# Low halves of the second feed-forward's down weights: from GpSimd subtractions to negated copies on ScalarE and accumulating DMAs

## What is computed

```
x = x + (1.0 + g1[:, None, :]) * rms_norm(y, post_norm_mix[l])
h = modulate(rms_norm(x, pre_norm_mlp[l]), sh2, sc2)
y = jnp.square(jax.nn.relu(h @ w_ff1[l])) @ w_ff2[l]      # w_ff1 1024 x 4096, w_ff2 4096 x 1024
x = x + (1.0 + g2[:, None, :]) * rms_norm(y, post_norm_mlp[l])
```

## Time and profile before

| what | us |
|---|---|
| three runs: median (lowest to highest) | 1814.74 (1811.52 to 1820.94) |
| the profiled execution | 1814.2 |
| its span, first to last instruction | 1812.5 |
| PE busy in the span | 1765.2 (97%) |
| POOL busy | 1037.3 (57%) |
| ACT busy | 780.8 (43%) |
| POOL's 1124 subtractions at L1003 | 911.6 |

### The profile page before, as it was taken

How to read it: one execution, slowest core, us unless ns; L and a number is a source line. 1 busy time by engine, 2 the same in 40 slices (tenths; PEclk the granted TensorE clock), 3 DMA queues, 4 the chain that set the end, 5 groups by cost and what they waited for, 6 DMA issues and landing times. The chain is left out here.

```text
span 1812.5 us, 26067 instructions
## 1 busy us (share of the span) xinstructions
PE 1765.2 (97%) x8977; PEld 1440.3 (79%) x8977; DVE 1122.1 (62%) x1826; ACT 780.8 (43%) x1270; POOL 1037.3 (57%) x1265
## 2 busy tenths in 40 slices
PE   8999999999999999999999999999999999999998
PEld 6876888888888886788888888877666778988886
DVE  4788656566656338766666655644476567655665
ACT  5434543333334335453333333466566663333332
POOL 6574445555465557364555554457311558888885
PEclk9999999999999999999999999999999999999999
DMA  7221224443423221133444332413201112233221
GB/s 253 94 102 50 82 82 151 150 151 115 150 93 117 93 98 54 48 105 112 144 162 148 130 115 82 140 49 118 92 1 48 47 47 94 94 117 114 96 93 47
DMA packets 103206, 184.70 MB, mean 102 GB/s; under 512 B 7322, under 2 KB 67404, under 8 KB 101068
## 3 DMA queue, kind: packets, MB, share of 16 engines
q1 hardware_dynamic: 102940, 183.44, 28.8%
q10 hardware_dynamic: 176, 0.07, 0.0%
HBM read 180.35 MB, written 2.10 MB: 101 GB/s over the span
## 5 line engine op out<-in xcount | busy, mean ns | idle before, releaser
L1003 POOL TENSOR_TENSOR w_lo<-raw,w_hi 128x256 fp32r<-128x256 f32 (+1 forms) x1124 | 911.6, 845 | 751.0 <-ACT w_hi L1089 747.5
L2499 PE MATMUL ps<-n_hi,w_hi 128*128 128x512 f32 (+1 forms) x1320 | 507.1, 384 | 3.9 <-ACT zc L1394 1.8
L2501 PE MATMUL ps<-n_hi,w_lo 128*128 128x512 f32 (+1 forms) x1320 | 501.1, 380 | 0.0
L2500 PE MATMUL ps<-n_lo,w_hi 128*128 128x512 f32 (+1 forms) x1320 | 500.7, 379 | 0.0
L1089 ACT ACTIVATE w_hi<-raw 128x1024 fp32r<-128x1024 f32 (+2 forms) x331 | 307.8, 937 | 359.6 <-PE ps L2501 240.8
L2499 PEld LDWEIGHTS ps<-n_hi,w_hi 128*128 128x128 f32 x1320 | 249.0, 189 | 53.1 <-issue 6.0
L2501 PEld LDWEIGHTS ps<-n_hi,w_lo 128*128 128x128 f32 x1320 | 249.0, 189 | 48.0
L2500 PEld LDWEIGHTS ps<-n_lo,w_hi 128*128 128x128 f32 x1320 | 249.3, 189 | 45.4 <-issue 0.2
L2043 DVE TENSOR_TENSOR ps<-ps,sq 128x512 f32<-128x512 f32 x88 | 61.3, 699 | 179.8 <-PE ps L2501 177.4
L2499 PE MATMUL ps<-x_hi,w_hi 128*128 128x512 f32 x416 | 167.0, 401 | 0.1
L2501 PE MATMUL ps<-x_hi,w_lo 128*128 128x512 f32 x416 | 162.6, 391 | 0.0
(11 more groups left out here) (359 smaller groups left out, 2668.5 us busy)
## 6 DMA issues: line engine op xcount, KB each, us to landing
raw<-in_w_up SPq DMA_DIRECT2D x44, 1024.0 KB, 6.9
raw<-in_w_ff SPq DMA_DIRECT2D x32, 1024.0 KB, 6.6
raw<-in_w_in SPq DMA_DIRECT2D x26, 1024.0 KB, 6.1
zb<-in_ada_w SPq DMA_DIRECT2D x16, 1536.0 KB, 8.3
raw<-in_w_down SPq DMA_DIRECT2D x44, 512.0 KB, 3.9
raw<-in_w_out SPq DMA_DIRECT2D x12, 1024.0 KB, 6.1
raw<-in_w_in SPq DMA_DIRECT2D x4, 512.0 KB, 8.2
za<-in_x SPq DMA_DIRECT2D x4, 512.0 KB, 6.1
```

Source lines behind the costliest of these rows:

```text
L1003: last = pool.tensor_tensor(part[0], part[1], part[2], ALU.subtract)
L2499: pe.matmul(out, l_hi, r_hi, start=start, stop=False)
L2500: pe.matmul(out, l_hi, r_lo, start=False, stop=False)
L2501: return pe.matmul(out, l_lo, r_hi, start=False, stop=stop)
```

## The change

For the 32 quarters of the eight ff2 stripes, POOL no longer subtracts. ACT, behind each high half, also writes the negated high half into `w_lo` (the same rounding copy with scale -1). POOL then issues a DMA inside SBUF that adds the raw weights to it (`accum_op=ALU.add`, 128 partitions x 2 rows of 512 float32, 512 KB), and waits for the DMA of the quarter before; a memset of one column of a new small tile `mark` then counts that quarter in `wlo_ready`. Two semaphores take turns for the DMAs. All other quarters are made as before.

```diff
--- before.py
+++ after.py
@@ -547,6 +547,7 @@
         t_const = sb("t_const", [P, 2 * S], F32R)
         sb("rest_of_const", [P, NCONST - P - 2 * S])
         swapped = sb("swapped", [P, 2, S])
+        mark = sb("mark", [P, 8])
         banks = ctx.enter_context(nc.psum_tensor("ps", [P, 8 * S], F32))
         ps = [banks[:, i * S:(i + 1) * S] for i in range(8)]
 
@@ -555,6 +556,7 @@
         free = [sem(f"free{i}") for i in range(8)]
         landed = [sem(f"landed{i}") for i in range(2)]
         whi_ready, wlo_ready = sem("whi_ready"), sem("wlo_ready")
+        wneg_ready, wadd_in = sem("wneg_ready"), [sem(f"wadd_in{i}") for i in range(2)]
         quarter_done = sem("quarter_done")
         ada_in, ada_used = sem("ada_in"), sem("ada_used")
         ident_in, consts_in, pos_in = sem("ident_in"), sem("consts_in"), sem("pos_in")
@@ -738,6 +740,9 @@
 
             return free[4 + i % 4], BK.ffn2[4 + i % 4] + 2 * (FG2 - 1) + i // 4 + 1
 
+        added_at = {g: n for n, g in enumerate(st.at[q] for st, q in by_quarter if st.kind == "H" and st.index >=
+                                               STR["ff2", 0].index)}
+
         def landed_value(st):
             return 32 * (st.index // 2 + 1)
 
@@ -978,12 +983,27 @@
             pool.memset(fgw[:, :, :], 1.0).then_inc(ones_set, 1)
             pool.memset(blkw[:, :, :, :], 0.0).then_inc(blk_zero, 1)
             pool.memset(swapped[:, :, :], 0.0).then_inc(swap_zero, 1)
+            def added(n):
+
+                pool.wait_ge(wadd_in[n % 2], 16 * (n // 2 + 1))
+                pool.memset(mark[:, n % 8:n % 8 + 1], 0.0).then_inc(wlo_ready, 1)
+
             def lo(g, value, used, pieces=range(LO_PARTS)):
 
                 st, q = by_quarter[g]
                 if st.kind == "S" and q == 6:
                     pool.wait_ge(last_lo, (st.index - STR["ff1", SEVEN_FROM].index) // 2 + 1)
                     pool.memset(small[:, 42:43], 0.0).then_inc(wlo_ready, 1)
+                    return
+                if g in added_at:
+                    n = added_at[g]
+                    pool.wait_ge(wneg_ready, n + 1)
+                    pool.dma_start(split_quarter(st.kind, w_lo.bitcast(F32), g % 4, q), source(st, q), accum_op=ALU.add)\
+                        .then_inc(wadd_in[n % 2], 16)
+                    if q:
+                        added(n - 1)
+                    if q == st.quarters - 1:
+                        added(n)
                     return
                 if pieces[0] == 0:
                     if used is not None:
@@ -1088,6 +1108,9 @@
                     act.wait_ge(quarter_done, used)
                 act.activation(split_quarter(st.kind, w_hi, g % 4, q), source(st, q),
                                ACT.Copy).then_inc(whi_ready, 1)
+                if g in added_at:
+                    act.activation(split_quarter(st.kind, w_lo, g % 4, q), source(st, q), ACT.Copy, scale=-1.0)\
+                        .then_inc(wneg_ready, 1)
 
             def ensure(upto):
                 for g in range(ahead[0], min(upto, len(by_quarter))):
```

## The result

The changed kernel took 1911.04 us (median of 4 runs, 1908.11 to 1918.02), the kernel before 1814.75 us (4 runs, 1811.52 to 1820.94): a ratio of 1.0532, 95% interval 1.0490 to 1.0574. The forecast was 1842.2 in a range of 1814 to 1862. The sign was right; the loss is 96 us where 28 were forecast. The profiled run was the longest of the four, 1918.0 us with a span of 1916.1, 103.6 more than the span before.

The account below looks back on a forecast made before the run. PE, busy for 1765.2 of the 1812.5 us span, was taken to bound the kernel. Losses of 6 x 4.4 + 1.6 = 28.0 us on the profiled 1814.2 gave 1842.2, 1.5% slower; range 1814 to 1862.

Parts of the forecast that it names:

- The step that failed: In an ff2 stripe, POOL issues quarter 0's DMA at 1712.8 and quarter 1's at 1714.4, once its negated copy is ready.
- when the data of an addition start: Beside SP's load, quarter 0's data start 1.36 us after issue, at 1714.1, and it is marked at about 1719.4.
- A load that goes first: Sign in the profile after: a gap above 3 us at PE's first matmul means this or a slow issue.
- rival B: Additions take 3.84 us of data each, or the load is served first: 7.0 us a period, 1860 us; chance 0.25.
- The data of an addition, 2.56 us: Each 512 KB accumulating DMA reads source and destination, so its data take 2.56 us where one pass takes 1.28.
- ACT costs nothing: The 32 negated copies on ACT, about 1.0 us each, fit into idle time of 1.75 us or more: cost 0.
- No gain in freed time of POOL: Removing 128 POOL subtractions, 12.98 us a period, frees nothing PE waits for; gain at most 2.5 us or 0.14%.
- 4.4 us for each of stripes 1 to 6: PE's loss in each such ff2 period: quarter 1 marked at 1724.5 against 1720.06, with 0.7 us late at quarter 0 included.
- The 0 for stripe 0: ff2 stripe 0 follows an ordinary ff1 stripe, so its negated copies are ready far earlier and it loses 0.
- Stripe 7: Last ff2 stripe, behind another ff2 stripe: quarter 3 lands at 1792.3 against 1790.75, 1.6 us late; quarters 0 and 1 have time.
- A, no change: The DMAs are as cheap as copies, 1.28 us of data each, so marks come in time: 1814.4 us; chance 0.19.
- C, the clock: Each 4.4 us stall brings PE 10 us at granted clock 0.83: 10 us on top, 1852 us; chance 0.06.

Follow-up runs that it names:

- long rows: Changed kernel with each addition taking 128 rows of 4 KB in place of 256 rows of 2 KB, the same 512 KB: 1865.8 us.
- the first experiment: Changed kernel with the addition left out, so the 32 DMAs of POOL are plain copies of the weights: 1848.4 us.
- the kernel with 14 additions and no stall: Changed kernel with additions only for quarters 2 and 3 of ff2 stripes 0 to 6, POOL subtracting the rest: 1815.35 us, ratio 0.9998.

## Why the prediction was wrong

**The step that failed** is "POOL issues the DMA of quarter 0 at 1712.8 ..., that of quarter 1 at 1714.4 (negated copy)". It let a second DMA out while the first was under way, with nothing but ACT's copy to wait for. The second was held until the first had landed, and the mark of quarter 0 behind it too. Of the 96 us, the hold is some 45: with it gone (long rows) the time is 1865.8 in place of 1911.0. These are single runs, and it depends on what is taken away first: with the load already moved the long rows give 48 (1877.3 against 1829.5), and by the losses against the kernel before on each chip it is 42 and 51. I had asked what the issue costs on POOL, between 0 and 3.25 us; it costs 1.21. I had not asked how many could be out at once.

**The second is when the data of an addition start** ("with equal shares and data from 1712.8 + 1.36 = 1714.1: quarter 0 has its 2.56 at 1719.2 and is marked at about 1719.4", 6.6 us after its issue). It was marked 11.9 us after. The DMA queues of the changed kernel from 1726 to 1730 us, and from 1730 to 1734 us (packets, MB, share of the 16 engines):

```profile
q1 hardware_dynamic: 516, 1.03, 92.0%
q0 software_dynamic: 1, 0.00, 0.3%
```

```profile
q0 software_dynamic: 240, 0.49, 65.7%
q1 hardware_dynamic: 301, 0.61, 43.9%
```

In the first four microseconds the load moved alone, at 259 GB/s where the kernel before moves 359 in the same four after its issue (1714.5 to 1718.5). The addition's packets come from about 1730 on, some 5.8 us after the issue and not 1.36. Once both ran, the share was even: 64 packets and 0.13 MB for each queue in every microsecond from 1731 to 1734. So of the 5.3 us by which the mark was later than forecast, 4.4 lie ahead of the first packets. "A load that goes first" stands in the prediction among what would show it wrong, but the prices put it under rival B. It isn't the adding and not the number of packets: the plain copy issued at 1586.30 beside the load has its first packets after 1591, the addition in long rows issued at 1592.44 after 1597. With no load beside it, the addition issued at 1599.34 is under way from 1601 on.

The Trainium skill, "DMA: Bandwidth & Descriptors", section "Queues, rings and completion order", says that each DMA engine takes turns between the queues that it has work for, packet by packet. The second stretch is in keeping with it (240 and 301 packets). The first (1 and 516) would speak against it only if the addition's packets were already waiting at the engines, which no run shows. Why a DMA of POOL starts so late beside a load wasn't tried and stays open.

The load beside the additions is worth some 36 us, 1865.8 against 1829.5 with it moved away (34 with the hold in place, 1911.0 against 1877.3; 39 and 30 by the losses on each chip).

**What was right.** *The data of an addition, 2.56 us.* Alone, an addition of 512 KB takes 3.66 us from the end of its issue to its mark (1.21 issue; 1747.63 to 1752.51 above). Alone, a plain copy takes 2.37, by its rows in the first experiment:

```profile
1509.10 0.73 POOL L1001 DMA_DIRECT2D w_lo<-raw  x1 [5.39 <-ACT w_lo L1112]
...
1512.20 0.10 POOL L989 MEMSET mark<- 128x1 f32 x1 [2.25 <-DMA w_lo<-raw]
```

The difference is 1.29 us, one more pass of 1.28; with the 1.36 fixed I had 3.92 where 3.66 was measured. By the rule of the two source reads, which the prediction cites from the Trainium skill, "Collectives: The Full Stack", section "The bandwidth ceiling: the fold count and why AG ≠ RS ≠ AR", an addition moves data half as fast as a copy, and the rows agree: 211 GB/s in a microsecond inside an addition alone (1738 to 1739 in the changed kernel), 418 inside this copy (1510.5 to 1511.5). *ACT costs nothing*, and the copies were ready when forecast: two activations of 1.06 and 1.04 us behind one another, with idle time left; the ratio of 1.0007 shows it. *The load starts in the same microsecond* (SP's issue at 1724.38, POOL's at 1724.25). *No gain in freed time of POOL*: the kernel with 14 additions and no stall has a ratio of 0.9998.

**The sum, term by term.** 4.4 us for each of stripes 1 to 6 was 8.7 to 10.1 us of wait, 54.7 together, and the slower clock behind it. Where the second DMA isn't held, PE's gaps are 4.12 and 0.36 us in one of the periods and some 4.9 on average (35.2 us in all, less 2.0 at stripe 0 and 3.8 at stripe 7, over six). That this is near 4.4 is luck: the forecast had 0.7 us in front of quarter 0 and 3.7 in front of quarter 1, it is the other way round, and the clock isn't in it. The 0 for stripe 0 was wrong: 5.7 us. Its copies were indeed ready early, but POOL issued the first DMA only at 1500.40, beside that stripe's load, and nothing in the prediction looked at when POOL gets there. Stripe 7 lost 6.0 us of wait, not 1.6, and 2.51 of them in front of quarter 1, which the forecast had at nothing:

```profile
1883.41 0.47 PE L2522 MATMUL ps<-w_hi,n_hi 128*128 128x512 f32 x1 [2.51 <-POOL mark L989]
```

The mark of quarter 1 stands behind the issue of quarter 2, which waited until 1881.94 for ACT's copy, and ACT for its slot. That is the order of the program and not the hold: with long rows, where nothing is held, the same wait is 2.11 us. The 1.43 us in front of quarter 2 are the hold: the issue of quarter 3, and the mark of quarter 2 behind it, waited for quarter 2 to land, and with long rows PE doesn't wait there. In front of quarter 3 it is 2.05 us, and 1.72 with long rows, where 1.6 was forecast: that term was right.

**The rivals.** A, no change, fell. B, three passes or a load served first, is partly what happened (its load, not its three passes), at 7.0 a period; its 1860 is close to the 1865.8 without the hold, but that run has the slower clock in it too, so the nearness proves nothing. C, the clock, was given 0.06 and came true in every period: PE stood still for 6 us and the granted clock went to 0.50, not to the mean of 0.83 of the earlier trace rows. Its price of 10 us on top is within the 8 to 14 that keeping the clock up gave back, by luck: the clock was lower than it assumed, and part of the slow matmuls cost nothing. The error there was the chance, since the forecast's own gap of 4.4 us was eight times the 0.58 us gap on which it was put so low; with long rows, behind a gap of 4.12 us, the granted clock from 1602 to 1604 us was 0.50. No rival had the hold, so the range ended at 1862.

## What to carry to other kernels

A DMA that takes a producer's place is priced by three questions, not one: how long does it take alone, what runs on the DMA engines in that very microsecond, and how many of its kind can be out at once. Here the third was answered in packets, so an addition is laid out in long rows (4 KB in these runs) or spread in time so that one lands before the next is due. And nothing urgent, such as the mark of the DMA before, stands behind a DMA instruction in program order: it waits for room, and for whatever that DMA waits for. And work taken off an engine that already idles bought nothing here: the only quarters for which the DMAs were harmless were those that nobody waited for.

## What the runs showed of the hardware

- A DMA instruction of POOL is held while there is no room for its packets, and the engine isn't: a memset ahead of it ran 9.5 us earlier. For additions the room lies between 432 packets (three DMAs of 144 went out) and 544 (two of 272 didn't). One addition counts a packet for each row of 1, 2 or 4 KB and 16 more; a plain copy of rows of 2 KB had 144 packets where the addition had 272. Whether copies are held at some number isn't shown.
- A DMA of POOL issued together with a load of SP (0.13 us apart in the changed kernel) has its first packets 4 to 6 us later, whether it adds or copies; without the load they are there within 2 us.
- The issue takes POOL 1.21 us with 272 packets, 0.88 with 144, and 0.72 for a copy.
- Additions move 512 KB at some 210 GB/s alone, and the length of the rows makes little difference: from the end of the issue to the mark 3.66 us for 512 KB in rows of 2 KB and 3.65 in rows of 4 KB (with a second one issued 2 us behind it), 2.4 to 2.5 for 256 KB in rows of 2 KB and of 1 KB. A plain copy of 512 KB takes 2.37. One microsecond inside an addition of the changed kernel, with nothing beside it:

```profile
1738.00:1739.00 1.00, 1.00 (x4) 0.81 (x3) 0.00 (x0) 0.00 (x0) 0.00 (x0) 0.50 1.15 211
```

- What the lower clock adds to PE's busy time isn't all lost: in the five periods PE was busy for 20.7 us more than before (231.6 against 210.9), and with the clock kept up the five periods were 6.1 us shorter (273.7 against 279.9).
